# A hybrid encoder layer with mixture of experts on one core: expert rows added in DRAM by accumulating scatters, and matmuls of constants at TensorE's waits

## The reference

```
g_idx  = argmax(u2 @ w_rg + b_rg)              # one of 4 groups
top2   = top_k((u2 @ w_re + b_re)[group], 2)   # two of the 8 experts of the group
w_pair = softmax(top2) * softmax(group)[g_idx]
y[tok] = sum over the pair of w_pair * (silu(x @ w_gate[e]) * (x @ w_up[e])) @ w_down[e]
out    = LN(alpha * x1 + (1 + gate(c)) * y) * ln2_g + ln2_b
```

## Time and profile before

| | us, or as named |
|---|---|
| median of 3 runs | 1540.34 (1537.71 to 1542.57) |
| span of the profiled execution | 1539.4 |
| loop over the 20 blocks, from the first L1875 to the last L1891 | 898.16 to 1483.75 |
| combining, to the end of DVE's last L2157 | 1483.75 to 1536.43 |
| loads of a heavy w_gate (the page, DMA issues) | 12: one before the loop, 11 in it |
| TensorE busy, all of the span | 1457.2 (95%) |
| mean granted TensorE clock | 0.972 |

### The profile page before, as it was taken

How to read it: one execution, slowest core, us unless ns; L and a number is a source line. 1 busy time by engine, 2 the same in 40 slices (tenths; PEclk the granted TensorE clock), 3 DMA queues, 4 the chain that set the end, 5 groups by cost and what they waited for, 6 DMA issues and landing times. The chain is left out here.

```text
span 1539.4 us, 19792 instructions
## 1 busy us (share of the span) xinstructions
PE 1457.2 (95%) x7307; PEld 810.2 (53%) x7308; DVE 566.3 (37%) x1134; ACT 357.4 (23%) x738; POOL 97.5 (6%) x97
## 2 busy tenths in 40 slices
PE   7999999989989899998999389999999999999987
PEld 4455554448868567664555354444444444444443
DVE  2222126567779334344877721011011011111118
ACT  1122122137634344442111111111111111111111
POOL 0000002000000000000000011111111111111110
PEclk9999999999999999999999579999999999999999
DMA  9401011128730200004111489969789879999965
GB/s 343 156 28 41 0 8 29 43 60 253 251 112 1 110 0 0 0 0 148 69 69 55 161 347 394 389 219 419 315 328 423 315 322 404 424 391 394 425 281 209
DMA packets 101798, 305.49 MB, mean 198 GB/s; under 512 B 18354, under 2 KB 61662, under 8 KB 92537
## 3 DMA queue, kind: packets, MB, share of 16 engines
q1 hardware_dynamic: 93064, 287.08, 48.5%
q0 software_dynamic: 8064, 16.80, 3.0%
q10 hardware_dynamic: 624, 1.03, 0.2%
HBM read 289.86 MB, written 25.76 MB: 205 GB/s over the span
## 5 line engine op out<-in xcount | busy, mean ns | idle before, releaser
L1891 PE MATMUL ps<-w_down_sb,hidT 128*128 x320 | 153.4, 612 | 0.0
L1875 PE MATMUL ps<-w_gate_sb,x_slotsT 128*128 x320 | 142.4, 598 | 0.4 <-ACT x_slotsT L1974 0.4
L453 PE MATMUL ps<-w_in_tok,uT 128*128 128x512 f32 (+2 forms) x384 | 141.5, 529 | 0.0
L1875 PE MATMUL ps<-w_up_sb,x_slotsT 128*128 x320 | 140.6, 592 | 0.0
L1551 PE MATMUL ps<-uT,hT 128*128 128x512 f32 x256 | 114.5, 601 | 0.0
L620 PE MATMUL ps<-uT,mod 128*128 128x512 f32 x256 | 112.7, 601 | 0.8 <-PEq L209 0.8
L2128 DVE TENSOR_TENSOR hid<-silu_g,ps 128x512 f32<-128x512 f32 x20 | 13.8, 688 | 259.0 <-PE ps L1875 259.0
L453 PEld LDWEIGHTS ps<-w_in_tok,uT 128*128 128x128 f32 x384 | 72.6, 190 | 65.5 <-issue 43.9
L1875 PEld LDWEIGHTS ps<-w_gate_sb,x_slotsT 128*128 128x128 f32 x320 | 61.4, 192 | 77.6 <-issue 77.6
L1875 PEld LDWEIGHTS ps<-w_up_sb,x_slotsT 128*128 128x128 f32 x320 | 60.8, 190 | 76.5 <-issue 76.5
L1891 PEld LDWEIGHTS ps<-w_down_sb,hidT 128*128 128x128 f32 x320 | 55.8, 189 | 65.1 <-issue 64.3
(11 more groups left out here) (403 smaller groups left out, 1875.1 us busy)
## 6 DMA issues: line engine op xcount, KB each, us to landing
light_gate_sb<-in_w_gate SPq DMA_DIRECT2D x20, 2048.0 KB
light_up_sb<-in_w_up SPq DMA_DIRECT2D x20, 2048.0 KB
light_down_sb<-in_w_down SPq DMA_DIRECT2D x20, 2048.0 KB
w_gate_sb<-in_w_gate SPq DMA_DIRECT2D x12, 2048.0 KB, 13.3
w_up_sb<-in_w_up SPq DMA_DIRECT2D x12, 2048.0 KB, 17.6
w_down_sb<-in_w_down SPq DMA_DIRECT2D x12, 2048.0 KB
mod<-in_w_ada SPq DMA_DIRECT2D x8, 1024.0 KB, 8.3
w_ada_late<-in_w_ada SPq DMA_DIRECT2D x8, 1024.0 KB, 6.8
```

The costliest lines, as they stand in the source:

```text
L453: mm = nc.tensor.matmul(ps[:, 2 + g, 0:n], self.uT[:, k, t * P:(t + 1) * P], wt[:, k, c0:c0 + n], start=k == 0, stop=k == KD - 1)
L1875: m = m_.matmul(ps[:, bank, :], xT[:, k, :], wt[:, bass.ds(buf, 1), k, :].rearrange("p a f -> p (a f)"), start=k == 0, stop=k == KD - 1)
L1891: m = m_.matmul(ps[:, 5 + half, :], hT[:, k, :], wd[:, bass.ds(buf, 1), k, half * 512:half * 512 + 512].rearrange("p a f -> p (a f)"), sta ...
```

## The change

There are two parts.

The first removes `ybuf` and the combining by PE. DVE multiplies each expert row by its pair's weight (divided by alpha) as well as by `gate2` (the instructions at L2138 and L2141 become `scalar_tensor_tensor`), and the two scatters add their rows onto the x1 rows in DRAM (`compute_op=ALU.add`), one after the other: the light one must land before the heavy one is issued. The bounds checks are gone. Empty places add onto 128 spare rows behind the 1024 (`x1d` has T + P rows), which SP clears at the start of the stage. The weights of the places are one more product of one-hot matrices on PE, before the loop (`at_w`), and three steps of copies on DVE. At the end SP loads the 8 summed tiles, DVE takes mean and variance and does the first of the two big operations; the second is split, the scale on ACT and the addition of `ln2_b` on POOL, for all tiles but the last.

The second part is `keep_clocked(bank, n)`: n matmuls of constants, 128x512 float32, into a PSUM bank that nobody reads, at twelve places of PE's stream.

```diff
-        self.x1d = d("x1_rows", (T, D))
-        self.ybuf = d("expert_rows", (2 * T, D))
+        self.x1d = d("x1_rows", (T + P, D))
...
+    def keep_clocked(self, bank, n):
+        for _ in range(n):
+            self.nc.tensor.matmul(self.ps[:, bank, :], self.c(C_ID), self.cst[:, 0:512], start=True, stop=True)
...
                 products(0)
+                self.keep_clocked(7, 3)
...
                 products(7)
+                self.keep_clocked(4, 4)
...
                     spread(k)
+                self.keep_clocked(2, 3)
...
                 turn(0)
+                self.keep_clocked(7, 2)
                 for t in range(TT):
                     products1(t, t % 2)
...
                     products2(t, t % 2)
+                self.keep_clocked(7, 1)
...
                 scores(0)
+                self.keep_clocked(6, 2)
...
                         if half:
+                            if t == 0:
+                                self.keep_clocked(7, 4)
                             pe.wait_ge(s_oan, t + 1)
...
                 logits(TT - 2)
+                self.keep_clocked(7, 8)
                 u2_turn(TT - 1)
...
+            srow, srowl = sb("sum_rows", [P, NB], I32), sb("light_sum_rows", [LC, NB], I32)
+            spare = sb("spare_row", [P, 1])
+            wsl, wsll, wslq = sb("slot_weights", [P, NCOL]), sb("light_weights", [LC, NB]), sb("light_quarter_weights", [P, NB])
...
-            at_row = [ys[:].rearrange("p (t q) -> p t q", t=TT), xT[:]]
+            at_row = [ys[:].rearrange("p (t q) -> p t q", t=TT), wd[:, 0, 0, :].rearrange("p (t q) -> p t q", t=TT)]
+            at_w = [wd[:, 0, 1 + k, 0:TT * NCOL].rearrange("p (t c) -> p t c", t=TT) for k in range(2)]
...
+                sp.wait_ge(s_x0, 2)
+                sp.dma_start(self.x1d[T:, :], xg[:]).then_inc(s_spare, 16)
...
-                sp.wait_ge(s_G, n + 1)
+                sp.wait_ge(s_lyfree, n + 1)
+                sp.wait_ge(s_yfree, n + 1)
                 for t in range(TT):
-                    sp.dma_start(x1[:, t], self.x1d[t * P:(t + 1) * P, :]).then_inc(s_x1[t], 16)
-                sp.wait_ge(s_yfree, n + 1)
-                sp.wait_ge(s_lyfree, n + 1)
-                for t in range(TT):
-                    sp.dma_start(yt(t), yb[t]).then_inc(s_y[t], 16)
-                for t in range(TT):
+                    sp.dma_start(rows[:, t], self.x1d[t * P:(t + 1) * P, :]).then_inc(s_sum[t], 16)
+                for t in range(TT - 1):
                     sp.wait_ge(s_o, t + 1)
                     sp.dma_start(self.out[t * P:(t + 1) * P, :], z[:, t]).then_inc(s_st, 16)
+                sp.wait_ge(s_last, 1)
+                sp.dma_start(self.out[(TT - 1) * P:, :], z[:, TT - 1]).then_inc(s_st, 16)
...
                 def scatter(b):
                     pool.wait_ge(s_lyd, b + 2)
-                    g.indirect_dma_start(out=yq, out_offset=bass.IndirectOffsetOnAxis(ap=asgq[:, b:b + 1], axis=0),
-                                         in_=yl[:], in_offset=None, bounds_check=quarter_end, oob_is_err=False).then_inc(s_lout, 16)
-                    pool.wait_ge(s_yd, b + 2)
-                    g.indirect_dma_start(out=self.ybuf, out_offset=bass.IndirectOffsetOnAxis(ap=smap[:, b:b + 1], axis=0),
-                                         in_=ys[:], in_offset=None, bounds_check=asg_end, oob_is_err=False).then_inc(s_out, 16)
+                    g.indirect_dma_start(out=sumq, out_offset=bass.IndirectOffsetOnAxis(ap=asgq[:, b:b + 1], axis=0),
+                                         in_=yl[:], in_offset=None, compute_op=ALU.add).then_inc(s_lout, 16)
                     pool.wait_ge(s_lout, 16 * (b + 1))
                     pool.sem_inc(s_lyfree, 1)
+                    pool.wait_ge(s_yd, b + 2)
+                    g.indirect_dma_start(out=self.x1d, out_offset=bass.IndirectOffsetOnAxis(ap=srow[:, b:b + 1], axis=0),
+                                         in_=ys[:], in_offset=None, compute_op=ALU.add).then_inc(s_out, 16)
                     pool.wait_ge(s_out, 16 * (b + 1))
                     pool.sem_inc(s_yfree, 1)
...
+                pool.wait_ge(s_spare, 16)
...
+                pool.wait_ge(s_dst, 6)
...
+                for t in range(TT - 1):
+                    pool.wait_ge(s_scaled, t + 1)
+                    g.tensor_tensor(z[:, t], z[:, t], self.b2[:], ALU.add).then_inc(s_o, 1)
...
+                self.keep_clocked(7, 8)
                 pe.wait_ge(s_A, 1)
                 Af = A[:].rearrange("p t e -> p (t e)")
...
                 m.then_inc(s_rank, 1)
+                self.keep_clocked(7, 8)
...
                 m.then_inc(s_rows, 1)
+                self.keep_clocked(7, 3)
...
+                self.keep_clocked(6, 2)
                 pe.wait_ge(s_xg, 16)
                 turn()
                 pe.wait_ge(s_lxg, 16)
                 turn_light(7)
+                for k in range(2):
+                    pe.wait_ge(s_hotw, k + 1)
+                    for t in range(TT):
+                        m = m_.matmul(ps[:, 5, 0:NCOL], at_row[k][:, t, :], at_w[k][:, t, :], start=k + t == 0, stop=k == 1 and t == TT - 1)
+                m.then_inc(s_Y, 1)
                 with turns(pe, n) as b:
...
-                def residual(t):
...
-                def rows_of_experts(t):
...
-                for t in range(TT):
-                    rows_of_experts(t)
-                    if t + 3 < TT:
-                        residual(t + 3)
...
-                    a.activation(ve[:, t % 2, 1:2], ve[:, t % 2, 0:1], ACT.Sqrt).then_inc(s_std, 1)
+                    a.activation(ve[:, t, 1:2], ve[:, t, 0:1], ACT.Sqrt).then_inc(s_std, 1)
+                    if t < TT - 1:
+                        act.wait_ge(s_gain, t + 1)
+                        a.mul(z[:, t], z[:, t], ve[:, t, 1:2]).then_inc(s_scaled, 1)
...
-                lk(v.tensor_tensor(self.wts[:, 0], sel[:], gw[:], ALU.mult))
+                lk(v.scalar_tensor_tensor(out=self.wts[:, 0], in0=sel[:], scalar=1.0 / ALPHA, in1=gw[:], op0=ALU.mult, op1=ALU.mult))
...
-                for q in range(4):
-                    v.tensor_scalar(asgq[q * LC:(q + 1) * LC, :], asgl[:], 4.0, float(q), ALU.mult, ALU.add).then_inc(s_lasg, 1)
...
+                for k in range(2):
+                    lk(v.tensor_tensor(at_w[k], self.c(C_IOTA, NCOL).unsqueeze(1).to_broadcast([P, TT, NCOL]), b3(colf[:, k], NCOL), ALU.is_equal))
+                    v.tensor_tensor(at_w[k], at_w[k], b3(self.wts[:, k], NCOL), ALU.mult).then_inc(s_hotw, 1)
+                lk(v.tensor_scalar_add(spare[:], self.c(C_PCOL, 1), float(T)))
+                v.tensor_scalar(srow[:], tok[:], spare[:, 0:1], None, ALU.min).then_inc(s_dst, 1)
+                v.tensor_scalar(srowl[:], tokl[:], spare[0:LC, 0:1], None, ALU.min).then_inc(s_dst, 1)
+                dve.wait_ge(s_dst, 2)
+                for q in range(4):
+                    v.tensor_scalar(asgq[q * LC:(q + 1) * LC, :], srowl[:], 4.0, float(q), ALU.mult, ALU.add).then_inc(s_dst, 1)
+                dve.wait_ge(s_Y, 1)
+                lk(v.tensor_copy(wsl[:], ps[:, 5, 0:NCOL]))
+                dve.sem_inc(s_yd, 1)
...
-                    v.tensor_tensor(yl[:], ps[:, 4, 256:256 + Q], gate2q[:], ALU.mult).then_inc(s_lyd, 1)
+                    v.scalar_tensor_tensor(out=yl[:], in0=ps[:, 4, 256:256 + Q], scalar=wslq[:, bass.ds(b, 1)], in1=gate2q[:], op0=ALU.mult, op1=ALU.mult).then_inc(s_lyd, 1)
                     dve.wait_ge(s_Y, b + 2)
                     dve.wait_ge(s_yfree, b + 1)
-                    v.tensor_tensor(ys[:].rearrange("p (a d) -> p a d", a=2), ps[:, 5:7, :], self.gate2[:].rearrange("p (a d) -> p a d", a=2), ALU.mult).then_inc(s_yd, 1)
+                    v.scalar_tensor_tensor(out=ys[:].rearrange("p (a d) -> p a d", a=2), in0=ps[:, 5:7, :], scalar=wsl[:, bass.ds(b, 1)],
+                                           in1=self.gate2[:].rearrange("p (a d) -> p a d", a=2), op0=ALU.mult, op1=ALU.mult).then_inc(s_yd, 1)
...
                 for t in range(TT):
-                    j, bank = t % 2, SUM_BANKS[t % 4]
-                    rows = ps[:, bank:bank + 2, :].rearrange("p a b -> p (a b)")
-                    dve.wait_ge(s_sum, t + 1)
-                    cb.link(v.bn_stats(st[:, 0, :], sums(t, 0)))
-                    cb.link(v.bn_stats(st[:, 1, :], sums(t, 1)))
+                    dve.wait_ge(s_sum[t], 16)
+                    cb.link(v.bn_stats(st[:, 0, :], rows[:, t, 0:512]))
+                    cb.link(v.bn_stats(st[:, 1, :], rows[:, t, 512:D]))
                     cb.link(v.bn_aggr(mv[:], st[:].rearrange("p a b -> p (a b)")))
-                    v.tensor_scalar_add(ve[:, j, 0:1], mv[:, 1:2], LN_EPS).then_inc(s_var, 1)
-                    v.scalar_tensor_tensor(out=z[:, t], in0=rows, scalar=mv[:, 0:1], in1=self.g2[:], op0=ALU.subtract, op1=ALU.mult).then_inc(s_read, 1)
-                    dve.wait_ge(s_read, t + 1)
+                    v.tensor_scalar_add(ve[:, t, 0:1], mv[:, 1:2], LN_EPS / ALPHA ** 2).then_inc(s_var, 1)
```

(6 more changed lines are left out.)

70 lines of the change are left out of this document (19 added, 51 removed).

## The result

The changed kernel takes 1547.53 us, the median of 5 runs (1545.29 to 1553.17), against 1540.34; the ratio is 1.0053, 95% interval 1.0035 to 1.0071. It is slower by 7 us where 7 us faster were forecast. The span of the profiled execution went from 1539.4 to 1545.6 us. Four stretches make this difference.

The account below looks back on a forecast made before the run. TensorE was taken to set the pace, busy 1457 of 1539 us. Ahead of the loop -10.7, loop +6, last stage -2.7: -7.4 on a span of 1539.4, so 1533 us by the median of runs, range 1512 to 1548.

Parts of the forecast that it names:

- The oan wait: Ahead of the loop, constants before the first oan wait raise the clock there and for the next products: -2.1 us.
- Attention: Ahead of the loop, constants at two attention places halve 3.30 and 3.45 us of half-clock PE work: -3.0 us.
- products(0): Ahead of the loop, three constants after products(0) halve 2.70 us of half-clock PE work at 253.60: -1.4 us.
- the end of mlstm: Ahead of the loop, constants halve PE's 2.92 us but can hold the barrier: -0.8 us (-1.5 to +1.2).
- the routing: From last tile to first block: higher clock, less 3.6 us for the weights' product: -3.4 us (-7 to +4).
- the 1 us of overlap: In the routing, some 1 us of the product of weights lies beside a wait for rows: -1.0 us.
- the upper bound: In the loop, old values pass the engines too: +17.8 MB, 49 us of engine time, 2.46 a turn.
- The last rival: In the loop, adding makes landings over 1.86 times as long, POOL's queue delays DVE and PE: 1605 us, chance 0.15.
- The hold: In the last stage, DVE's L2154 waits for POOL's addition: period 5.1 us, DVE ends 2.7 us sooner.
- No hold: Rival: in the last stage POOL's addition passes beside DVE, 12.8 us less: 1520 (1512 to 1525), chance 0.22.
- POOL's chain: The last rival: light scatter, heavy scatter and two gathers exceed a loop turn, +72 us at 2.2 times, chance 0.15.
- Absorbed: Rival: clock rises, but other engines or loads are late and constants outlast waits: 1540 (1537 to 1547), chance 0.13.

Follow-up runs that it names:

- the two other traces without constants: The kernel before with POOL waiting for the light landing before issuing the heavy scatter, 1539.05 us; and the changed kernel with all constant matmuls deleted, 1557.12 us.
- constants only: The kernel before with the twelve places of constant matmuls alone, its combining unchanged: 1534.88 us, ratio 0.9973.
- The run with plain writes: The changed kernel with scatters that write instead of adding, same number, order and bytes: 1534.63 us, ratio 0.9960.
- the run without POOL: The changed kernel without POOL's additions of `ln2_b` for seven tiles, ACT's result being stored: 1533.63 us, ratio 0.9954.

## Why the prediction was wrong

The sum was -7.4 on the span; +6.2 was measured. The misses are 6.1 us ahead of the loop, 4.3 in the loop and 3.2 behind it. The measured 1547.53 lies inside the stated 1512 to 1548, but by luck: that end was set for a chain on POOL that just exceeds its turn, and the chain did not come.

*Ahead of the loop, -10.7 forecast, -4.55 measured: a term each.* The oan wait gave -2.1 as forecast (-3.13 at the end of attention to -5.26 at the first L1560). Attention gave -3.2 against this trace of before, for -3.0, but the two other traces without constants gain 0.8 and 1.2 in the same stretch by themselves, so between -2.0 and -3.2 is due to the constants. products(0) gave -1.7 from L634 to the mlstm stage, for -1.4 forecast; another -0.5 stood there at L634 already, where the two without constants stand at -0.6 and -0.9. Little of it outlives mlstm: at 418 us the changed kernel is at -0.63, inside the 0 to -1.09 of the kernels without constants.

What failed is the step that constants hide in a wait. At the end of mlstm, where I forecast -0.8, the changed kernel loses 0.7 us from the stage's last PE instruction, L981, to L1256 (lines of the kernel before), and the other seven traces with all these constants do the same; the two with none lose 0.3. The next stage's first PE instruction (L1240) loses 2.1 us (from -0.63 to +1.46), and 1.4 are given back behind it. The three runs without these constants gain 1.4, 0.5 and 0.5 there. Behind products(7) the constants brought the next stretch forward, and 1.6 us were lost up to 418, some of it at 355 to 360, where the clock fell anew: the matmuls on `w_ada_late` there take 1.80 us in the changed trace, 1.07 before. In the routing I forecast -3.4 and got +0.7, for two reasons that share it. Eight constants were priced at 0.89 us each, at full clock; they took 9.95 us together and held the counting, which stood 2.0 us sooner in the trace where they took 7.11; five held the turn of the rows with 6.56 us. Against all constants, fewer of them gave 4.3 us more in the loop's start, of which 2.2 at the end of mlstm and 2.1 in the routing. The other reason is the product of weights, 3.8 us in the open, for 3.6 forecast; but the 1 us of overlap that I took off did not exist: L1889 follows without a gap and L1899 follows it. The constants only kernel, without this product, stands 4.1 us better at the same place.

*The loop, +6 forecast, +10.25 measured: the mechanism was right and the size was off.* The adding cost engine time as if the old values pass the engines, so the upper bound was the right one: +49 us of engine time, 51 measured. Its parts were a little off and cancelled: 13 us for the empty places and 36 for the adding were reckoned; the run with plain writes has 57 us over its span, which makes them about 10 and 41. I took +6 near the middle of 1 to 14, with no row for it. With the upper bound the three full turns give 3 x 2.46 = 7.4, and PE's waits grew by 8.1, from 1.1 to 9.2 us. The run with plain writes puts the difference on the adding alone: stall 0.5 us instead of 8.8. The Trainium skill's rule in Collectives: The Full Stack (The bandwidth ceiling: the fold count and why AG ≠ RS ≠ AR), two source reads for an add and about half the rate, told there of a ring of cores, fits the 2.2 times of engine time. It does not carry over to the landings, as the prediction let it: they grew 1.44 times, not twice. The last rival therefore did not come. The sum also lacked a second charge: 2.1 us of low clock behind a wait of 8.8. The place was off too: 2 to 3 us in each of the three full turns were forecast, but these took 29.12, 29.12 and 29.64, and the turn behind them 39.96. All other turns stayed at 29.1.

*The last stage, -2.7 forecast, +0.5 measured.* The hold was right, price and place: 3.01 to 3.12 us a piece, period 4.88 against my 5.1, which gave 1.5 us. But I let tile 0 start 9.6 us behind the last `y_slots` and it started 12.74 behind. I had set the smaller tile against the slower landing. They don't balance. The last light scatter landed 3.6 and the last heavy one 6.0 us after issue, instead of the shortest 2.1 and 3.2 of the earlier trace rows, and since the heavy one waits for the light one it was issued only at 1492.83, 3.3 us behind the start of `y_slots` instead of 1.5: 4.6 us lost, of which the smaller loads gave back 1.6. With plain writes the same stage starts 3.9 us sooner. At the end the sum had nothing for POOL's DRAIN, which took 1.5 us more.

*The rivals.* "No hold" was refuted in the trace and in the run without POOL. "POOL's chain" was refuted in price, by 21.0 us of landings. "Absorbed" was the nearest in mechanism, as constants outlasting their waits was in it. Its time was added up wrongly: -4, +9 and -2.7 to +5.7 make +2.3 to +10.7, which is 1543 to 1551 and not 1540 (1537 to 1547). Rightly added it holds the measured 1547.5. Its losses were weighed as a small chance together; each was likely by itself.

## What to carry to other kernels

Matmuls that keep the clock up are priced at the clock which they meet, and behind idle time that can be the low one: the same eight took 7.11 us in one execution and 9.95 in another. So give each wait fewer than its length at full clock would hold, look for a small rest of waiting at the consumer in more than one trace, and give none to the end of a stage whose barrier they could hold. A transfer that adds in DRAM cost about 2.2 times the engine time of one that writes; here, where loads fill the DMA engines for three turns on end, nearly the whole surplus came out as one stall, and the clock was low behind it. An operation given to POOL held DVE's operation with two SBUF operands until POOL was done: it cost DVE 1.74 us of POOL's 2.34, and only the small operations passed beside it. Compare one trace with another only where other traces of the same stream agree.
